# Third transpose buffer, VectorE copies in the short attention pairs, and columns in pieces at the end of a two-block transformer on one core

## Time and profile before

| | us |
|---|---|
| three runs | 3219.55, 3216.07, 3219.4 (median 3219.4) |
| the profiled execution, its own time | 3216.57 |
| its span, first to last instruction | 3214.8 |
| TensorE matmul busy | 3101.8 (96%) |
| VectorE, ScalarE, GpSimd busy | 1476.5, 1200.7, 396.6 |
| mean granted TensorE clock | 0.988 |

### The profile page before, as it was taken

One profiled execution on the slowest core, in us unless ns is written; L12 is line 12 of the kernel. 1 busy time (PEld: TensorE's weight loads), 2 busy tenths in 40 slices (PEclk: granted clock), 3 DMA queues, 4 the chain that ended last, 5 costly groups with the idle time before them and its releaser, 6 DMA issues.

```text
span 3214.8 us, 42841 instructions
## 1 busy us (share of the span) xinstructions
PE 3101.8 (96%) x16934; PEld 2536.8 (79%) x16934; DVE 1476.5 (46%) x2224; ACT 1200.7 (37%) x1836; POOL 396.6 (12%) x616
## 2 busy tenths in 40 slices
PE   8999998999999999999999999999999999999997
PEld 6888887787778878888888778557778788888886
DVE  6652357666653435524533532565454322222233
ACT  4651138877663233312212331465442311212121
POOL 0110007655542000000000000120010000000000
PEclk9999998999999999999999999999999999999999
DMA  3222320000004211111111131001102111111111
GB/s 139 83 79 75 110 80 8 2 1 2 1 1 152 90 46 48 50 46 52 46 46 52 46 129 46 21 2 33 40 14 98 46 46 52 46 51 47 46 52 65
DMA packets 49898, 168.02 MB, mean 52 GB/s; under 512 B 8816, under 2 KB 9968, under 8 KB 49376
## 3 DMA queue, kind: packets, MB, share of 16 engines
q1 hardware_dynamic: 38784, 125.96, 11.7%
q0 software_dynamic: 10976, 40.15, 3.5%
HBM read 143.54 MB, written 16.78 MB: 50 GB/s over the span
## 4 chain that ended last, share of the span: by engine, by line
PE 90%; ACT 4%; DVE 3%; issue 2%; POOL 1%; DMA 0%; DVEq 0%; ACTq 0%; SPq 0%; POOLq 0%
PE PS L226 70%; PE PS L859 3%; PE PS L845 3%; PE PS L241 3%; PE PS L830 2%; PE PS L829 2%; PE PS L1617 1%; PE PS L1644 1%; PE PS L1629 1%; ACT PT L938 1%; ACT P_SHORT L928 1%; PE PS L880 1%; DVE PT L1027 1%; PE PS L871 0%; PE PS L315 0%
## 5 line engine op out<-in xcount | busy, mean ns | idle before, releaser
L199 ACT CAST WHI<-RAW 128x1024 fp32r<-128x1024 f32 x219 | 230.3, 1052 | 1355.0 <-PE PS L226 1334.3
L204 DVE TENSOR_TENSOR WLO<-RAW,WHI 128x1024 fp32r<-128x1024 f32 x219 | 268.7, 1227 | 1001.9 <-ACT WHI L199 1001.6
L226 PE MATMUL PS<-HLO,WHI 128*128 128x512 f32 x2160 | 667.5, 390 | 0.0
L226 PEld LDWEIGHTS PS<-HLO,WHI 128*128 128x128 f32 x2160 | 406.9, 188 | 85.1
L226 PE MATMUL PS<-X_HI,WHI 128*128 128x512 f32 x1504 | 467.4, 392 | 4.5 <-DVE W L336 2.2
L226 PE MATMUL PS<-X_HI,WLO 128*128 128x512 f32 x1504 | 464.7, 390 | 0.0
L226 PEld LDWEIGHTS PS<-X_HI,WHI 128*128 128x128 f32 x1504 | 282.4, 189 | 66.9 <-DVE W L2137 2.6
L226 PEld LDWEIGHTS PS<-X_HI,WLO 128*128 128x128 f32 x1504 | 283.6, 189 | 59.4
L226 PE MATMUL PS<-HID_HI,WHI 128*128 128x512 f32 x864 | 266.7, 390 | 6.4 <-DVE HID_LO L1349 6.4
L226 PE MATMUL PS<-HID_HI,WLO 128*128 128x512 f32 x864 | 266.4, 390 | 0.0
L226 PE MATMUL PS<-HID_LO,WHI 128*128 128x512 f32 x864 | 266.4, 390 | 0.0
(11 more groups left out here) (334 smaller groups left out, 4548.8 us busy)
## 6 DMA issues: line engine op xcount, KB each, us to landing
RAW<-in_w SPq DMA_DIRECT2D x219, 512.0 KB, 3.3
X<-in_x SPq DMA_DIRECT2D x8, 512.0 KB, 7.8
Q<-QN POOLq DMA_DIRECT2D x32, 128.0 KB, 2.7
merged<-W POOLq DMA_DIRECT2D x8, 512.0 KB, 3.1
W<-gate POOLq DMA_DIRECT2D x8, 512.0 KB, 4.0
W<-merged POOLq DMA_DIRECT2D x8, 512.0 KB, 4.7
X<-in_x POOLq DMA_DIRECT2D x8, 512.0 KB, 10.7
x_kept<-X POOLq DMA_DIRECT2D x8, 512.0 KB, 7.6
```

The costliest lines, as they stand in the source:

```text
L199: nc.scalar.copy(WHI[:, slot, :], RAW[:, slot, :]).then_inc(w_hi, 1)
L204: nc.vector.tensor_tensor(WLO[:, slot, :], RAW[:, slot, :], WHI[:, slot, :].bitcast(F32), ALU.subtract).then_inc(w_lo, 1)
L226: last = nc.tensor.matmul(o[:, half], w[:, slot, cols], x(k)[:, half], start=(k == 0 and w is WHI and x is hi), stop=(done and k == kcs - ...
```

## The change

1. `pe_first_units` waits part by part: the high x high matmuls for the weights' and tile's high parts, the others for the low parts. On an otherwise waiting TensorE three fp32 matmuls of 512 columns of zeros run first; VectorE writes the zeros.
2. In attention there are three transpose banks instead of two; the two output tiles share one bank, so a pair's values wait until the pair before is copied out (`o_free`). ScalarE's output copies and VectorE's subtraction for pair m-1 move ahead of the first batch's copies and of the compressed branch's steps.
3. In pairs with one batch (query tiles 0 to 3) VectorE copies every second group.
4. The first two down-units of feed-forward 1's last group do tiles 0 to 4 each, then tile 5 each.
5. The last two units are done in pieces of 512, 256 and 256 columns; adding, squares, mean, root, scaling (into a tile `Y`) and sending are done by piece.

```diff
@@ pe_first_units, step @@
             for w, x in ((WHI, hi), (WHI, HLO), (WLO, hi)):
+                if x is HLO:
+                    pe.wait_ge(h_ready, 8 * n + k + 1)
+                elif w is WHI:
+                    pe.wait_ge(w_hi, u + b + 1)
+                    pe.wait_ge(hhi_done, 8 * n + k + 1)
+                else:
+                    pe.wait_ge(w_lo, u + b + 1)
...
-        pe.wait_ge(w_lo, u + 1)
...
@@ attention @@
-    T_PS = [PS[:, 2 * T + 512 * i:2 * T + 512 * i + 512] for i in range(2)]
-    O_PS = [PS[:, 3 * T + 512 * i:3 * T + 512 * i + P] for i in range(2)]
+    T_PS = [PS[:, c:c + 512] for c in (2 * T, 2 * T + 512, 3 * T + 512)]
+    O_PS = [PS[:, 3 * T + P * i:3 * T + P * i + P] for i in range(2)]
-    def dve_copies(batch, i):
+    def dve_copies(m, batch, i):
+        if len(batches_of(m)) == 1:
+            return i % 2 == 1
         return batch[0] > 0 and (i - batch[0]) % 2 == 0
@@ pe_turn (pe_cmp_turn and pe_cmp_scores alike) @@
-        if c >= 2:
-            wait_copied(pe, c - 2)
+        if c >= 3:
+            wait_copied(pe, c - 3)
@@ pe_cmp_values @@
-        if m >= 2:
-            pe.wait_ge(o_free, m - 1)
+        if m:
+            pe.wait_ge(o_free, m)
@@ act_attention @@
+            if m:
+                act_out_hi(act, m - 1)
             for i in b[0]:
-                act_copy(act, m, i)
+                if not dve_copies(m, b[0], i):
+                    act_copy(act, m, i)
             if ahead:
                 if len(b) == 1:
                     act_exp(act, 2 * ahead, 0)
                 act_exp(act, 2 * ahead, 1)
-            if m:
-                act_out_hi(act, m - 1)
@@ dve_attention, behind the first head's two minima @@
+            if m:
+                dve_out_lo(dve, m - 1)
+            if len(b) == 1:
+                for i in b[0][1::2]:
+                    dve_copy(dve, m, i)
             if m in SUMMED:
                 dve_cmp_sum(dve, SUMMED[m])
...
-            if m:
-                dve_out_lo(dve, m - 1)
@@ pe_ff1 @@
-        for b in range(2):
-            pe_unit_at(pe, U_Z2 - KC + b, 0, hi, lo, FF1_REST, None if b else tile_ready)
+        for part in range(2):
+            for b in range(2):
+                u = U_Z2 - KC + b
+                j = jobs_before(u)
+                if not part:
+                    pe.wait_ge(w_lo, u + 1)
+                    pe.wait_ge(evacuated, j - 1)
+                product(pe, u % 2, j % 2, hi, lo, FF1_REST - 1 + part, 0, None if b else tile_ready,
+                        part * (FF1_REST - 1), part == 1)
@@ pe_ff2, the last two units @@
+        for i, (a0, a1) in enumerate(END_COLS):
+            for b in range(2):
...
+                for k in range(KC):
+                    if i and b == 0 and k == 4:
+                        pe_end_mean(pe, i - 1)
...
+        pe_end_mean(pe, 2)
@@ dve_ff2, behind the sixth of the last units @@
+        dve_end_add(dve, 0)
+        dve_end_add(dve, 1)
+        dve_end_scale(dve, 0)
+        dve_end_add(dve, 2)
+        dve_end_scale(dve, 1)
+        dve_end_scale(dve, 2)
@@ SyncE @@
-        for k in range(KC):
-            sp.wait_ge(y_done, k + 1)
-            sp.dma_start(out[k], X[:, k, :]).then_inc(out_done, 16)
+        for i, (a0, a1) in enumerate(END_COLS):
+            for k in range(KC):
+                sp.wait_ge(y_done, KC * i + k + 1)
+                sp.dma_start(out[k][:, a0:a1], Y[:, k, a0:a1]).then_inc(out_done, 16)
@@ TensorE, first @@
+        pe.wait_ge(dve_seq, 1)
+        for _ in range(3):
+            nc.tensor.matmul(SIDE[1][:, 0:512], W[3][:, 0:P], W[3][:, 0:512], start=True, stop=True)
```

More of the change, by code:

```diff
@@ L875, in pe_cmp_scores @@
         qt, g = s // 2, s % 2
-        if s and c_scored_at[s] >= 2:
-            wait_copied(pe, c_scored_at[s] - 2)
-        out = T_PS[c_scored_at[s] % 2] if s else C0_PS
+        if s and c_scored_at[s] >= 3:
+            wait_copied(pe, c_scored_at[s] - 3)
+        out = T_PS[c_scored_at[s] % 3] if s else C0_PS
         for h in range(HPG):
@@ L998, in act_attention @@
                 for i in b[1]:
-                    if not dve_copies(b[1], i):
+                    if not dve_copies(m, b[1], i):
                         act_copy(act, m, i)
@@ L2192, in dve_ff2, with dve_end_add, dve_end_scale @@
             tiles(U_LAST_UP, 2 * p, GROUP * (FF2_GROUPS - 1) + 2 * p + 2, 2 * p + 2)
-        dve_residual(dve, U_LAST, 4, XB, lambda t: XB[:, t, :], lambda t: None)
+        for t in range(KC - 2):
+            if t:
+                dve_acc(dve, 4, t - 1)
+            dve_add_residual(dve, U_LAST + t, 0, XB, t)
+            dve_split(dve, U_LAST + t + 2)
+        dve_acc(dve, 4, KC - 3)
+        dve_end_add(dve, 0)
[4 more added lines that the diff above has]
+        dve_end_scale(dve, 2)
+    def dve_end_add(dve, i):
+        a0, a1 = END_COLS[i]
+        for b in range(2):
+            x = XB[:, KC - 2 + b, a0:a1]
+            dve.wait_ge(job_done, J_END + 2 * i + b + 1)
+            nc.vector.tensor_tensor(x, x, end_sums(b, i), ALU.add).then_inc(evacuated, 1)
+        dve.wait_ge(acc_done, 7 * 4 + 6 + i)
+        dve.wait_ge(sq_done, 8 * 4 + 6 + 2 * i + 1)
+        nc.vector.tensor_tensor(ACC[:, a0:a1], ACC[:, a0:a1], SQ[0][:, a0:a1], ALU.add).then_inc(acc_done, 1)
+    def dve_end_scale(dve, i):
+        a0, a1 = END_COLS[i]
+        dve.wait_ge(rstd_done, 4 + i + 1)
+        dve.wait_ge(evacuated, J_END + 2 * i + 2)
+        for k in range(KC):
+            nc.vector.scalar_tensor_tensor(Y[:, k, a0:a1], XB[:, k, a0:a1], NORM_W[:, 4, k:k + 1],
+                                           RSTD[4][:, a0:a1], ALU.mult, ALU.mult).then_inc(y_done, 1)
     def pe_ff2(pe):
@@ L2211, in pe_ff2, with pe_end_mean @@
             pe_unit_at(pe, U_LAST + b, 0, hi, lo, ready=None if b else tile_ready)
-        with pe.Fori(1, KC // 2) as t:
+        with pe.Fori(1, KC // 2 - 1) as t:
             for b in range(2):
                 pe_unit_at(pe, U_LAST + b, 2 * t, hi, lo)
-    def dve_final(dve):
-        dve.wait_ge(rstd_done, 5)
-        for k in range(KC):
-            nc.vector.scalar_tensor_tensor(X[:, k, :], XB[:, k, :], NORM_W[:, 4, k:k + 1], RSTD[4][:, :],
-                                           ALU.mult, ALU.mult).then_inc(y_done, 1)
+        for i, (a0, a1) in enumerate(END_COLS):
+            for b in range(2):
+                if i == 0:
+                    pe.wait_ge(w_lo, UNITS - 1 + b)
+                    pe.wait_ge(evacuated, J_END - 1 + b)
+                for k in range(KC):
+                    if i and b == 0 and k == 4:
+                        pe_end_mean(pe, i - 1)
+                    cols = slice(k * P, (k + 1) * P)
+                    for w, x in ((WHI, hi), (WHI, lo), (WLO, hi)):
+                        last = nc.tensor.matmul(end_sums(b, i), w[:, (UNITS - 2 + b) % 2, cols], x(k)[:, a0:a1],
+                                                start=(k == 0 and w is WHI and x is hi),
+                                                stop=(k == KC - 1 and w is WLO))
+                last.then_inc(job_done, 1)
+        pe_end_mean(pe, 2)
+    def pe_end_mean(pe, i):
+        a0, a1 = END_COLS[i]
+        pe.wait_ge(acc_done, 7 * 4 + 7 + i)
+        pe.wait_ge(sq_done, 8 * 4 + 6 + 2 * i + 2)
+        nc.tensor.matmul(SIDE[0][:, a0:a1], ONES[:, :], ACC[:, a0:a1], start=True, stop=False)
+        nc.tensor.matmul(SIDE[0][:, a0:a1], ONES[:, :], SQ[1][:, a0:a1], start=False, stop=True)\
+            .then_inc(mean_done, 1)
+    Y = sb("Y", [KC, T], H_AT + 32 * KB)
     block_cm = nc.Block()
```

48 lines of the change are left out of this document (30 added, 18 removed).

## The result

The changed kernel took 3194.9 us in the median of four runs (3193.4 to 3197.2), the kernel before beside it 3217.7 (3215.2 to 3219.6): a ratio of 0.9929, 95% interval 0.9914 to 0.9944. It is faster by 22.8 us, where 44 were forecast, and lies above the range's upper end of 3191. Its profiled execution took 3197.2, span 3195.4 against 3214.8.

A forecast was written before the change was run, and what follows sets the result against it. TensorE was taken as the bound, so only its idle places give time back. Terms 2.1 + 26.2 + 4.5 - 1.5 + 6.5 + 6.0 = 43.8 us off the 3219.4 median gave 3175 us, range 3161 to 3191.

The forecast's parts named there:

- Short pairs: Attention's short pairs: moving 32 copies from ScalarE to VectorE levels the load and saves 4.5 us, ends -6 and 13.
- Rival 1: Short pairs: VectorE's queue takes the place of ScalarE's as what is late; 3187 us, chance 15%.
- One bank for both outputs: Attention: a pair's output waits until the pair before is copied out; cost 0, worked out on a long pair.
- The cover of 0.8 us: Long pairs: shared bank free at 792.6, TensorE asks at 793.4; cost arises only if the copies slip.
- Rival 5: Long pairs: shared output bank comes free 2.8 us past its cover, 32 x 2.8 = 90, 3265 us; chance 2%.
- Long pairs: Attention's 32 long pairs: a third transpose buffer removes waits for copies and saves 26.2 us, ends 13 and 28.
- Handover: From short to long pairs: copies and output subtractions ahead of VectorE's sum cost 1.5 us, ends 0 and 3.
- Start: First product: finer waits and dummy products bring the first mean from 28.36 to 26.3, saving 2.1 us, ends 0 and 2.1.
- Tail: First feed-forward's end: new tile order fills the 6.43 us wait; saves 6.5 us, ends 4.5 and 7.
- End: Last two units in pieces of 512, 256 and 256 columns save 6.0 us, ends 3.5 and 7.5.
- VectorE's copies and GpSimd: Attention: copies out of PSUM cost GpSimd nothing; the opposing rival, copies block GpSimd's late gates, 3195 us, had 3%.

The follow-up runs named there:

- kernel 8: Kernel 1 with both output copies back in their late places in the long pairs, from pair 33 on; 3258.8 us.
- kernel 1: Changed kernel with short pairs (0 to 31) as before: two transpose banks, two output banks, late output copies, every copy on ScalarE; 3170.2 us.
- kernel 11: Kernel before the change with only the change's start, feed-forward tail and end; all of attention as before; 3202.7 us.
- kernel 4: Kernel 1 with both output copies (ScalarE's and VectorE's) early in the short pairs; 3182.0 us.
- kernel 5: Kernel 1 with VectorE making the copies of every second group in the short pairs (31 of the 32); 3190.6 us.
- kernel 6: Changed kernel, short pairs keeping three transpose buffers and the shared output bank, but with output copies late and every copy on ScalarE; 3267.7 us.
- kernel 10: Kernel 1 with the new feed-forward tail, the end in pieces and the dummy products at the start undone; 3187.3 us.
- kernel 3: Changed kernel, short pairs with two transpose buffers and two output banks, early output copies and VectorE's copies kept; 3209.6 us.

## Why the prediction was wrong

**Short pairs: the step that failed.** They were forecast to gain 4.5 us and lost 27.1. The two traces together fall 24.4 us short of the sum and not 31.6, as the long pairs, the handover, block 2 and the end came out better. The forecast said: "32 copies of 0.588 us leave ScalarE and cost VectorE 0.692 each", "the load is levelled, not removed", 4.5 gained, ends -6 and 13. It summed the busy time of each engine in a stage and took what was left over as room. The runs show that the room was no room: TensorE, VectorE and ScalarE pass each pair around in a fixed order, and an instruction that waits holds back those behind it on its queue. Freed ScalarE time did not come back; 31 copies taken away from it cost 20.5 us on otherwise unchanged pairs (16.6 in these pairs and the handover by the traces), and in the last place tried 2.2 us each. The low end of -6 was a quarter of a microsecond per pair, chosen with no row behind it, while the earlier trace rows showed that a late copy costs TensorE its wait. Rival 1 named this mechanism. Its 10.5 is counted from the 4.5 gained, so its price against no copies was 6, a third of what they measure alone.

**One bank for both outputs: cost 0 was right where it was worked out, and never worked out elsewhere.** The cover of 0.8 us came from a long pair, whose scores and first batch separate the copy from the next values. In a short pair VectorE comes to the subtraction behind the turn before, with its selection and queries, and little of TensorE's work lies between. I counted the exchange for 32 long pairs and applied the edit to 64. Rival 5 gave the mechanism, but put it in the long pairs; the wait of up to 3.4 us came in the short ones. I gave it no chance there. Its price, 2.8 against 2.86 in kernel 8, agrees in part by luck, as the wait itself is 2.2 and the clock makes the rest.

**The early place of the output copies was taken as free.** It costs 0.4 us a pair in both kinds of pairs: 11.9 in the short ones, 12.1 in the long.

**Long pairs: 29.1 against 26.2, right, with one part that I had not seen.** Kind by kind the sum holds: 0.5, 1.0 and 0.5 us a pair with five, six and seven groups, where 0.4, 0.9 and 0.45 stood, and 1.3 and 2.0 to 2.1 for 1.3 and 1.8 with the compressed branch. Not seen was the price of the early place, 12.1 with two buffers. The third buffer hides it, as it hides the old waits: 44.6 less 12.1 is 32.5 by medians, of which 29.2 lie between pairs 32 and 63. That this price did not show in the net was not worked out; there it was luck.

**Handover: -1.0 against +1.5.** The 9.46 us from the minimum to the transposes were forecast well (9.3). But pair 31's values, where the stretch begins, were themselves 2.5 us late for the subtraction, which shortens it. With the old banks and places it is 10.55 (kernel 1) to 12.03 (kernel 11), and with early copies 13.55 (kernel 4). Of these 3 us between kernels 1 and 4 only 0.7 is standing still; the rest is a granted clock of 0.76 in that stretch, 1.00 in kernel 1 and 0.89 in kernel 11. So the term of 1.5 can't be told from the clock.

**Start: 1.35 against 2.1.** The floor was right and was 0.3 us later in this run: VectorE ends the sum at 25.39 + 1.21 = 26.60, and TensorE reached the mean 0.4 behind it. In kernels 1, 5, 6, 8 and 10 the mean waits for the sum, at 27.2 to 28.4, whatever is gained ahead of it. The same start gives 26.6 to 28.4 in the traces, so 1.35 and 2.1 can't be told apart.

**Tail: 6.6 against 6.5**, with the wait for weights forecast at 1.3 and measured at 1.18. By the means 5.0 against the kernel before and 6.9 in kernel 10. **End: 7.2 against 6.0**, the same to 0.1 in all pairs of traces.

**VectorE's copies and GpSimd.** No run shows the gates held up: GpSimd's gate products in the short pairs have a mean of 676 ns in the changed kernel, where VectorE copies 32 groups, and 676 in the kernel before and 671 in kernel 1, where it copies none. Only 12 of the 128 run beside such a copy for over 0.1 us, and none of them is longer than its like. The Trainium skill, SBUF — State Buffer, section Who interferes with whom, lets a copy block GpSimd only where its operands meet the conditions of a mode that takes the shared ports; these copies, out of PSUM, show no such block.

**How sharp the measure is.** Unchanged block 2 takes from 596.3 (kernel 1) to 602.7 us (kernel 3) in the fourteen traces. Its windows in kernel 1, the changed kernel and kernel 3:

```profile
1865.03:2461.29 596.26, 568.57 (x3401) 437.88 (x3400) 283.19 (x455) 252.15 (x394) 50.80 (x161) 0.99 0.13 43
1889.43:2489.29 599.86, 571.64 (x3401) 439.61 (x3400) 283.06 (x455) 252.28 (x394) 51.15 (x161) 0.98 0.12 43
1902.13:2504.86 602.73, 574.69 (x3401) 441.54 (x3400) 283.08 (x455) 252.28 (x394) 50.60 (x161) 0.98 0.12 43
```

TensorE stands still for 27.7 to 28.2 us in all three; what differs is how long the same matmuls take, with the granted clock. The first feed-forward shows it row by row. Behind the same wait of 2.23 us its pairs of matmuls take 0.61 in the kernel before (first line) and 1.05 for some 3 us in the changed one (second), which is the +1.6 of the table:

```profile
1195.99 0.61 PE L226 MATMUL PS<-X_HI,WHI 128*128 128x512 f32 x2
...
1192.00 1.05 PE L226 MATMUL PS<-X_HI,WHI 128*128 128x512 f32 x2
```

Why the clock falls in one and not in the other stays open. It limits what one trace can say of a long stretch to some 3 us, and 3.6 of kernel 1's 24.7 against the change are of this kind; so were the 2.6 of block 2 that the changed kernel gained without an edit. The short stages are compared by themselves, and 27.2 us of them came back in kernel 1.

## What to carry to other kernels

Where several engines hand a small tile around, idle time on one is not room for work: find for each new instruction what it waits for and what stands behind it, in each kind of iteration that the edit reaches, not only in the kind it was made for. Before a bank is taken from one use for another, look in every kind of iteration at when its remaining use is released; here the right form was the exchange in the long pairs alone (3170.2 instead of 3194.9). A gain and a cost that hide each other are found only by kernels that have one of them.

## What was not expected of the hardware

In these runs idle time costs twice: in the changed kernel's short pairs TensorE needs 167.6 us for the work that takes it 160.5 in kernel 1, at granted clocks of 0.87 and 0.94. With the bank shared and the copies late (kernel 6) it needs 191.3, at 0.78 (window over nearly all its short pairs):

```profile
485.00:758.70 273.70, 191.34 (x1440) 169.91 (x1436) 122.99 (x458) 146.84 (x413) 124.02 (x169) 0.78 0.00 1
```

The clock's rise at the start moves by more than three dummy products can be seen to change: with the same code there the pairs of matmuls reach their short time of 0.62 to 0.69 anywhere from 11.6 us (kernel 6) to 15.0 (kernel 11), and without the dummies at 12.0.
